# Four of eight weight remainders per pair of up-projection tiles: from VectorE to GpSimd

## The reference, cut to what matters

```python
up = x @ w_up                      # 1024 -> 2 * 2816
h = conv_b + sum(padded[:, j:j + T] * conv_w[j] for j in range(3))
val, gate = jnp.split(h, 2, axis=-1)
out = (jax.nn.silu(gate) * val) @ w_down   # 2816 -> 1024
```

## Time and profile before

| | us |
|---|---|
| three runs | 1274.96, 1274.01, 1271.08 (median 1274.01) |
| profiled execution, its own time | 1272.19 |
| its span, first to last instruction | 1270.3 |
| PE busy, share of the span | 1231.9, 97% |
| DVE busy | 824.6, 65% |
| ACT busy | 504.7, 40% |
| POOL busy | 167.5, 13% |
| mean granted TensorE clock, share of full | 0.99 |

### The profile page before, as it was taken

The page is one execution under the profiler, slowest core; times in us unless marked ns, Lnnn a source line. Parts: engine busy times, 40 slices in busy tenths (PEclk is TensorE's granted clock), DMA queues, the critical chain, the costliest instruction groups (busy, mean ns, idle before and its releaser), DMA issues.

```text
span 1270.3 us, 20299 instructions
## 1 busy us (share of the span) xinstructions
PE 1231.9 (97%) x7964; PEld 1189.9 (94%) x7964; DVE 824.6 (65%) x1476; ACT 504.7 (40%) x800; POOL 167.5 (13%) x143
## 2 busy tenths in 40 slices
PE   7999999999899999999999999999999999999995
PEld 7988888999899999999999999999999999999984
DVE  6796766575787647688645764577457853478444
ACT  5411111234456425656522542254225551255335
POOL 5210000000000035210020002000200022000352
PEclk9999999999999999999999999999999999999998
DMA  7431322527423521221263136312631136311412
GB/s 267 118 116 44 84 69 78 169 85 160 104 77 119 198 106 34 90 79 55 82 217 118 52 77 221 121 52 76 210 135 52 53 87 214 118 46 45 165 69 97
DMA packets 82894, 138.49 MB, mean 109 GB/s; under 512 B 24992, under 2 KB 50592, under 8 KB 82792
## 3 DMA queue, kind: packets, MB, share of 16 engines
q1 hardware_dynamic: 82800, 137.21, 33.7%
HBM read 96.67 MB, written 39.50 MB: 107 GB/s over the span
## 4 chain that ended last, share of the span: by engine, by line
PE 83%; DVE 9%; ACT 3%; issue 2%; DMA 1%; POOL 1%; SPq 0%; ACTq 0%; DVEq 0%; POOLq 0%
PE psum L1728 47%; PE psum L1477 14%; PE psum L1496 5%; PE psum L1544 4%; PE psum L1617 3%; PE psum L1833 2%; PE psum L1595 1%; PE psum L1468 1%; DVE SC L2154 1%; PE psum L1591 1%; DMA raw<-in_w_dn 1%; PE psum L1579 1%; DVE K L2144 1%; DVE QP L2145 1%; PE psum L1555 1%
## 5 line engine op out<-in xcount | busy, mean ns | idle before, releaser
L1728 PE MATMUL psum<-XH,wh 128*128 128x344 f32 x688 | 219.9, 320 | 1.1 <-ACT ub L1225 1.0
L1728 PE MATMUL psum<-XH,wl 128*128 128x344 f32 x688 | 219.7, 319 | 0.0
L1728 PE MATMUL psum<-XL,wh 128*128 128x344 f32 x688 | 219.7, 320 | 0.0
L1433 POOL TENSOR_TENSOR wl<-raw,wh 128x512 fp32r<-128x512 f32 (+2 forms) x36 | 57.6, 1600 | 590.7 <-ACT wh L1174 578.8
L1728 PEld LDWEIGHTS psum<-XH,wh 128*128 128x128 f32 x688 | 129.3, 188 | 1.6 <-issue 1.6
L1728 PE MATMUL psum<-AH,wl 128*128 128x344 f32 x408 | 130.4, 320 | 0.0
L1728 PE MATMUL psum<-AL,wh 128*128 128x344 f32 x408 | 130.4, 319 | 0.0
L1728 PE MATMUL psum<-AH,wh 128*128 128x344 f32 x408 | 130.3, 319 | 0.0
L1728 PEld LDWEIGHTS psum<-XH,wl 128*128 128x128 f32 x688 | 129.2, 188 | 0.0
L1728 PEld LDWEIGHTS psum<-XL,wh 128*128 128x128 f32 x688 | 129.0, 188 | 0.0
L1728 PE MATMUL psum<-TR,wh 128*128 128x344 f32 x480 | 126.8, 319 | 0.0
(11 more groups left out here) (342 smaller groups left out, 2573.3 us busy)
## 6 DMA issues: line engine op xcount, KB each, us to landing
raw<-in_w_up SPq DMA_DIRECT2D x44, 512.0 KB, 3.9
RS<-rscr SPq DMA_DIRECT2D x16, 516.0 KB, 4.4
rscr<-RS SPq DMA_DIRECT2D x16, 516.0 KB, 3.8
raw<-in_w_units SPq DMA_DIRECT2D x15, 512.0 KB, 4.3
raw<-in_w_dn SPq DMA_DIRECT2D x24, 256.0 KB, 3.0
fscr<-st SPq DMA_DIRECT2D x10, 516.0 KB, 2.9
raw<-in_w_dn SPq DMA_DIRECT2D x16, 320.0 KB, 3.3
R<-in_xT SPq DMA_DIRECT2D x8, 516.0 KB, 7.4
```

The costliest lines, as they stand in the source:

```text
L1433: pool.tensor_tensor(dst, src, high.bitcast(F32), ALU.subtract).then_inc(w_lo, 1)
L1728: ins = nc.tensor.matmul(psum[:, bank, 0:CW], a[:, k * P:(k + 1) * P], x, start=(start and p_ == 0), stop=(stop and p_ == 2), skip_group_c ...
```

## The change

The remainders of S1, A21, S4 and A22 of each of the pairs 2 to 21 are formed by GpSimd instead of VectorE. `low_up` returns at once for these four, and `lo` forms them in the order of `JOBS`, between the remainders of plain and down tiles. Whoever waits for one of them waits on `w_lo` now; the counts of both semaphores are numbered anew. Shapes, operands, slots and the other engines' streams stay.

```diff
+POOLED = ("S1", "A21", "S4", "A22")
...
-LO_COUNT = {w: i + 1 for kinds in (("combo",), ("tile", "down", "last")) for i, w in enumerate(w for w in JOBS if w[0] in kinds)}
+
+
+def on_pool(w):
+
+    return w[0] != "combo" or w[2] in POOLED
+
+
+LO_COUNT = {w: i + 1 for where in (False, True) for i, w in enumerate(w for w in JOBS if on_pool(w) == where)}
...
-            return (c_lo if w[0] == "combo" else w_lo), LO_COUNT[w]
+            return (w_lo if on_pool(w) else c_lo), LO_COUNT[w]
...
                 pool.wait_ge(w_hi, HI_COUNT[w])
-                if kind == "tile":
+                if kind == "combo":
+                    i = COMBOS.index(x)
+                    dst, high = half(wl, i), half(wh, i)
+                    src = raw_half(x) if x[0] == "A" else half(WS, i)
+                elif kind == "tile":
...
             for w in JOBS:
-                if w[0] != "combo":
+                if on_pool(w):
                     lo(w)
...
             def low_up(j, x):
-
+                if x in POOLED:
+                    return
                 dve.wait_ge(w_hi, HI_COUNT["combo", j, x])
```

## The result

The changed kernel takes 1279.6 us (median of six runs, 1278.0 to 1283.7), the kernel before 1271.4 (six runs, the first three of them those of the table above, 1268.8 to 1275.0). The medians are 8.2 us apart. The estimate of the ratio is 1.0072, with a 95% interval of 1.0056 to 1.0088: 7.1 to 11.2 us slower. The forecast was slower, by 13.6 us; the direction and the place are right, the size is above the whole interval, and the time lies 1.4 us under the range.

What follows compares the result with a forecast made beforehand. TensorE was taken as the bound. Fifteen stalls of 0.83 us at P6 (12.5 us) plus 1.1 us in pair 2 gave 13.6 us on a median of 1274.0, so 1287.6 us, range 1281 to 1297.

Steps and rivals of the forecast that it cites:

- What bounds the kernel; relief is worth nothing: Up- and down-projection: TensorE is the bound; relieving another engine can shorten these stages by no more than about 1 us.
- GpSimd in time: The 80 moved remainders, 1.30 us each on GpSimd, are ready before TensorE needs them; lateness costed at nothing.
- The hold and where it falls: In `conv(j, 0)`, S4's and A22's remainders alternate with VectorE's instructions, delaying ScalarE's take of P1 and so P6, fifteen times.
- The size of the hold: In `conv(j, 0)`: 1.05 us for S4 and 1.25 for A22, 2.3 together, bounds 2.1 to 2.6; stall 0.83 us.
- The cover: At P6, 1.47 us of delay to the take of P1 is absorbed before PE stalls.
- Pair 2: `conv(1, 1)` begins 1.2 us earlier, is held 2.3 us; T3's low part for P7 comes later, costing 1.1 us.
- The base: The whole kernel's median before the change, 1274.0 us, to which the predicted 13.6 us was added.
- The first: Rival: in `conv(j, 0)` A22's remainder comes only after L2399, hold 1.05 us, no stall; 1274 to 1275 us, chance 0.11.
- The second: Rival: no hold to speak of, VectorE freer, PE's wait in pair 2 goes; 1273.0 us, chance 0.05.
- The third: Rival: each remainder holds VectorE 1.8 us, `c21` included, 3.6 a stage; 34 us at the far end, chance 0.11.

Runs made afterwards that it cites:

- E0: Not a run: one of TensorE's groups of matmuls, right before P6 in the kernel before; no time of its own is given.
- three holds: The changed kernel with one more GpSimd subtraction of 344 columns between S4's and A22's remainders of each pair; ratio 1.0168.
- the control: The kernel before, unchanged, run once more for a second profile; one run, 1269.8 us.

## Why the prediction was right in kind and wrong in size

**What bounds the kernel; relief is worth nothing.** Right. With S1 and A21 alone on GpSimd VectorE is busy 16.3 us less, and the time is the same.

**GpSimd in time.** Right: no wait of PE for `wl`, and none when two of them came nearly 3 us later.

**The hold and where it falls.** Right, with the gaps as forecast: one gap after the other.

**The size of the hold, the step that failed.** I took "1.25 us, the 1.30 less a short overlap" for the second hold, and 2.3 us for both, with 2.1 as the lower bound. Measured are 0.99 and 2.03, under the bound. The row of before already had the answer: L2396 ended at 640.85, GpSimd at 640.82. With its own 0.22 us the VectorE instruction must have begun in effect at 640.63, some 0.2 us before GpSimd's end. I used this in the first hold without noticing (1.05 is a difference of two measured times) and not in the second. The same 0.2 us is in the changed kernel: L2411 ended at 707.38, less 1.28 is 706.10, and GpSimd ended at 706.30. Issued 0.10 us after GpSimd, it is held 1.29 - 0.10 - 0.20 = 0.99 us. The bounds that I set for this hold were no bounds: 1.30 is the length of an instruction and 1.05 the hold of the first gap, and neither is worked out from when the second VectorE instruction is issued and when it can go on. The stall at P6 was so forecast at 0.83 us and came out at 2.03 - 1.47 = 0.56.

**The cover.** Right: 1.47 us forecast. TensorE at P6 of pair 6 in the changed kernel, the last matmuls of E0 and the first of P6:

```profile
707.34 0.32 PE L1740 MATMUL psum<-XL,wh 128*128 128x344 f32 x1
707.50 0.32 PE L1740 MATMUL psum<-XH,wl 128*128 128x344 f32 x1
708.22 0.55 PE L1740 MATMUL psum<-TR,wh 128*128 128x344 f32 x2 [0.40 <-ACT ub L1233]
708.61 0.32 PE L1740 MATMUL psum<-TR,wl 128*128 128x344 f32 x1
708.77 0.48 PE L1740 MATMUL psum<-TR,wh 128*128 128x344 f32 x2
709.08 0.32 PE L1740 MATMUL psum<-TR,wl 128*128 128x344 f32 x1
```

Matmuls start 0.16 us apart, so P6 was due at 707.66 and began 0.56 us late: the hold of 2.03 less the cover of 1.47. With three holds it begins 1.23 us late, and 2.71 - 1.47 is 1.24. One term was missing from the sum: the first two matmuls behind a wait take 0.39 us to the third start, where others take 0.31. This adds 0.08 us a stage. Fourteen stages at 0.56, pair 3 at 0.84 and fifteen times 0.08 make 9.9 us where 12.5 was forecast.

**Pair 2.** 1.1 us forecast. PE's wait for T3's low part rose from 0.2 to 0.5 us, and the wait before P3 stayed (1.0 us). So it cost 0.3, and the term was wrong in what VectorE regains. The conv of pair 1's gate half in the changed kernel:

```profile
573.62 1.28 DVE L2408 SCALAR_TENSOR_TENSOR hb<-ub,cp,hb 128x1024 f32<-128x1024 f32 x1 [1.17 <-ACT hb L1227]
```

And in the control:

```profile
575.67 0.69 DVE L2381 TENSOR_TENSOR wl<-WS,wh 128x512 fp32r<-128x512 f32 x1 [1.08 <-ACT wh L1174]
576.28 0.68 DVE L2381 TENSOR_TENSOR wl<-raw,wh 128x512 fp32r<-128x512 f32 x1
576.88 1.28 DVE L2395 SCALAR_TENSOR_TENSOR hb<-ub,cp,hb 128x1024 f32<-128x1024 f32 x1
```

In the changed kernel it begins as soon as ScalarE's evacuation ends (573.59), in the control 1.76 us after that end (575.12). It regains 1.7 us and not the 1.2 of the two remainders, since VectorE no longer waits for S4's high part in front of them. Against a hold of 2.0 us, 0.3 is left.

These terms make 10.2 us; between the changed kernel's stretch and the control's there are 9.9.

**The base.** Of the miss of 8.0 us (1287.6 against 1279.6), 2.6 are not in the change. I set 13.6 us on a median of three runs, 1274.0, and six have 1271.4; with 29 more runs of the same kernel the median is 1270.5, with a spread from 1267.7 to 1275.0. A range from 1281 upward left no room for that. Between the two profiles, too, the stretch grew by 11.5 us while the span grew by 5.7, since the part before it happened to be 5.3 us shorter. The control, whose stretch is 9.9 us shorter than the changed kernel's, and which has the same wait at E0, is the comparison that holds.

**The rivals.** The first, a second remainder behind the conv, would have been no loss. The A22-only kernel is in effect this case, one hold of 1.04 under the cover, and it did cost nothing. The second fell with the first L2409 of 1.26 us. The third, more held, counted on a renewed queueing, of `c21` with its operand in PSUM too; such instructions aren't held (last section), and the holds stayed at 1.04 and 0.99 us.

## What to carry to other kernels

The engines do not meet only at semaphores, as I put it at the start: VectorE and GpSimd hold each other up in mid-conv, with no semaphore between them. So moving work to an idle engine is not free: price it as the time that the busy engine is held, instruction by instruction, at the place where it will run, and set that against the cover of the next semaphore. Here the remainders of S1 and A21 cost nothing, one hold of 1.04 us in the conv costs nothing, and two cost 0.6 us each time. The cure is a place or a cover: start the moved work behind the conv that is waited for, or put one more group of matmuls ahead of the one that waits.

Set a small predicted difference on a base of more than three runs, and read a hold from two end times, not from a duration.

## What the runs showed of the hardware

- GpSimd's two-input subtraction and VectorE's two-input instructions take turns, one for one, also in gaps of instructions that were queued back to back (three gaps, three holds of 1.04, 0.64 and 1.03 us).
- VectorE goes on about 0.2 us before the recorded end of the GpSimd instruction that held it (640.63 against 640.82; 706.10 against 706.30), if its own length is taken to be what it is alone.
- GpSimd's memset, which reads nothing, neither holds VectorE nor is held: 0.22 and 1.28 us as ever, with four memsets of 485 to 496 ns each.
- A VectorE instruction with one operand in PSUM neither is held nor holds. The changed kernel's down stage shows it, VectorE's instruction first, then GpSimd's, overlapping by 0.52 us, each at the length that it has alone:

```profile
653.07 1.23 DVE L2493 SCALAR_TENSOR_TENSOR ub<-ub,psum 128x1032 f32<-128x1032 f32 x1 [4.45 <-PE psum L1740]
```

```profile
653.78 1.30 POOL L1445 TENSOR_TENSOR wl<-raw,wh 128x512 fp32r<-128x512 f32 x1 [1.88 <-ACT wh L1182]
```
